# A new layout of the on-chip memory: operands of the dense products below 128 KiB of a partition, most of the rest above

## The reference

```python
# block 1: cond = silu(c); mod = cond @ ada_w + ada_b
h = modulate(rmsnorm(x, norm_mix), sh1, sc1)
x = x + g1 * diff_attention(h, ...)        # 8 heads, softmax(s1) - lam * softmax(s2)
h = modulate(rmsnorm(x, norm_ffn), sh2, sc2)
x = x + g2 * hier_moe(h, ...)              # 16 experts, D -> 512 -> D, two chosen per token
x = rmsnorm(x, norm_final)
# block 2
h = rms_norm(x); x = x + even_mixer(h)     # forgetting attention and multiscale pooling
h = rms_norm(x); x = x + conv_ffn(h)       # D -> 2 x 2816 -> D, convolution of width 3
h = rms_norm(x); x = x + conformer_conv(h) # pointwise, 31 taps, layer norm, pointwise
h = rms_norm(x); x = x + conv_ffn(h)
```

## Time and profile before

| | |
|---|---|
| median of 3 runs | 1865.18 us (1861.98 to 1866.87) |
| span of the profiled execution, first to last instruction | 1865.3 us |
| PE busy | 1803.2 us, 97% of the span, 8492 matmuls |
| PEld, DVE, ACT, POOL busy | 75%, 65%, 49%, 10% |
| mean granted TensorE clock | 0.985 |
| HBM traffic | 143 GB/s over the span |

### The profile page before, as it was taken

The page is one execution under the profiler, slowest core; times in us unless marked ns, Lnnn a source line. Parts: engine busy times, 40 slices in busy tenths (PEclk is TensorE's granted clock), DMA queues, the critical chain, the costliest instruction groups (busy, mean ns, idle before and its releaser), DMA issues.

```text
span 1865.3 us, 26168 instructions
## 1 busy us (share of the span) xinstructions
PE 1803.2 (97%) x8492; PEld 1399.4 (75%) x8492; DVE 1217.4 (65%) x1892; ACT 918.1 (49%) x1402; POOL 186.5 (10%) x219
## 2 busy tenths in 40 slices
PE   7999989899999789999999999999998999999999
PEld 5777667788888667767788888887764788888887
DVE  6777684798898672454577777224898567777422
ACT  3566652578788534564444444215665534444220
POOL 0000000222322100001000000000774000000000
PEclk9999999799999989999999999999999999999999
DMA  9533132999999451110232323321210223332321
GB/s 401 186 94 100 57 124 80 339 361 374 379 372 373 166 199 46 46 46 23 81 102 100 98 93 104 110 90 57 69 59 32 80 79 94 97 101 90 122 92 57
DMA packets 73074, 259.74 MB, mean 139 GB/s; under 512 B 10416, under 2 KB 10544, under 8 KB 71728
## 3 DMA queue, kind: packets, MB, share of 16 engines
q1 hardware_dynamic: 68400, 250.47, 38.5%
q0 software_dynamic: 4608, 8.40, 1.2%
HBM read 254.63 MB, written 12.59 MB: 143 GB/s over the span
## 4 chain that ended last, share of the span: by engine, by line
PE 85%; DVE 6%; issue 4%; ACT 2%; DMA 2%; DVEq 0%; SPq 0%; POOL 0%; POOLq 0%; ACTq 0%
PE ps L1016 18%; PE ps L1018 18%; PE ps L1017 18%; PE ps L1256 3%; PE ps L1257 3%; PE ps L1258 3%; PE ps L1078 2%; PE ps L1276 2%; PE ps L1278 1%; PE ps L1277 1%; PE ps L1099 1%; PE ps L1037 1%; PE ps L1039 1%; PE ps L1038 1%; PE ps L1473 1%
## 5 line engine op out<-in xcount | busy, mean ns | idle before, releaser
L1016 PE MATMUL ps<-h_hi,w_hi 128*128 128x512 f32 x1120 | 448.4, 400 | 1.2 <-DVEq L2267 1.2
L1018 PE MATMUL ps<-h_hi,w_lo 128*128 128x512 f32 x1120 | 437.4, 391 | 0.0
L1017 PE MATMUL ps<-h_lo,w_hi 128*128 128x512 f32 x1120 | 436.9, 390 | 0.0
L124 DVE TENSOR_TENSOR w_lo<-raw,w_hi 128x1024 fp32r<-128x1024 f32 x212 | 266.0, 1258 | 185.4 <-ACT w_hi L119 185.2
L119 ACT ACTIVATE w_hi<-raw 128x1024 fp32r<-128x1024 f32 x212 | 221.5, 1050 | 200.1 <-PE ps L1018 163.9
L1016 PEld LDWEIGHTS ps<-h_hi,w_hi 128*128 128x128 f32 x1120 | 210.7, 188 | 71.5 <-issue 28.4
L1018 PEld LDWEIGHTS ps<-h_hi,w_lo 128*128 128x128 f32 x1120 | 210.6, 188 | 44.4
L1017 PEld LDWEIGHTS ps<-h_lo,w_hi 128*128 128x128 f32 x1120 | 210.9, 188 | 43.9 <-issue 2.4
L163 DVE TENSOR_TENSOR w_lo<-ring,w_hi 128x1024 fp32r<-128x1024 f32 x128 | 149.6, 1219 | 29.4 <-ACT w_hi L159 29.4
L900 ACT ACTIVATE tmp<-ps,param 128x512 f32<-128x512 f32 x88 | 68.7, 780 | 184.7 <-DVE ps L2233 184.7
L2241 DVE SCALAR_TENSOR_TENSOR tmp<-ps,param,tmp 128x511 f32<-128x511 f32 (+1 forms) x176 | 131.8, 749 | 18.9 <-DVE tmp L2241 3.0
(11 more groups left out here) (345 smaller groups left out, 2936.8 us busy)
## 6 DMA issues: line engine op xcount, KB each, us to landing
ring<-in_w_m SPq DMA_DIRECT2D x192, 512.0 KB, 5.4
raw<-in_w_b SPq DMA_DIRECT2D x180, 512.0 KB, 3.5
raw<-in_w_a SPq DMA_DIRECT2D x32, 512.0 KB, 3.6
ada_late<-in_ada_b SPq DMA_DIRECT2D x32, 512.0 KB, 4.2
ada<-in_ada_a SPq DMA_DIRECT2D x8, 1024.0 KB, 20.7
y_tok<-y_dram SPq DMA_DIRECT2D x8, 512.0 KB, 6.9
x<-in_x SPq DMA_DIRECT2D x2, 1024.0 KB, 6.8
h_dram<-h_tok SPq DMA_DIRECT2D x4, 512.0 KB, 2.6
```

What stands on the lines that cost most here:

```text
L124: dve.tensor_tensor(self.lo[:, s, :], self.raw[:, s, :], self.hi[:, s, :].bitcast(F32), ALU.subtract).then_inc(self.lo_done, 1)
L1016: pe.matmul(dst, hi, a_hi, start=first, stop=False, skip_group_check=True)
L1017: pe.matmul(dst, hi, a_lo, start=False, stop=False, skip_group_check=True)
L1018: return pe.matmul(dst, lo, a_hi, start=False, stop=last, skip_group_check=True)
```

## The change

No instruction, wait, size or order is changed: both programs have the same instructions in the same order on each engine. Only where tensors lie is new. `ring` is now a list of 8 slots (`ring_h`, over `h_hi` and `h_lo`) and the 4 slots of `raw`; `ada` is a list of 5 parts low and 3 parts high. Offsets in KiB of a partition, as the two programs allocate them:

| tensor | before | after |
|---|---|---|
| w_hi, w_lo | 92 to 124 | 16.1 to 48.1 |
| h_hi, h_lo | 44 to 76 | 51.9 to 83.9 |
| a_hi, a_lo | 135.8 to 167.8 | 83.9 to 115.9 |
| c_hi | 194 to 210 | 83.9 to 99.9 |
| c_lo | 178 to 194 | 99.9 to 115.9 |
| gv_hi | 135.8 to 179.8 | 83.9 to 127.9 |
| gv_lo | 179.8 to 223.8 | 179.8 to 223.8 |
| m_hi, m_lo | 199.9 to 215.9 | 83.9 to 99.9 |
| e_hi, e_lo | 171.8 to 179.8 | 99.9 to 107.9 |
| hid_hi, hid_lo | 183.8 to 187.8 | 107.9 to 111.9 |
| e_x (two), e_hid | 167.8 to 219.9 | 111.9 to 123.9 |
| v | 157.8 to 173.8 | 83.9 to 99.9 |
| wf_hi, wf_lo | 196.6 to 197.1 | 208.6 to 209.1 |
| glu, diag | 135.8 to 162 | 115.9 to 126.2 |
| const | 16.1 to 24.9 | 127.9 to 136.7 |
| x | 28 to 44 | 139.8 to 155.8 |
| tmp | 124 to 132 | 155.8 to 163.8 |
| junk | 132.8 to 133.8 | 48.9 to 49.9 |
| raw | 76 to 92 | 163.8 to 179.8 |
| ring, 12 slots | 44 to 92 | 51.9 to 83.9 and 163.8 to 179.8 |

The added allocations, in their order, with the lines that stay the same left out:

```diff
+ADA_NEAR = 5
...
-        sp.dma_start(self.ring[:, c], self.src[bass.ds(i, 1), c]).then_inc(self.loaded[c][0], 16)
+        sp.dma_start(self.ring[c], self.src[bass.ds(i, 1), c]).then_inc(self.loaded[c][0], 16)
...
-        const = sb("const", [P, CONST.n])
-        param = sb("param", [P, PARAM.n])
-        x = sb("x", [P, KC, T])
-        with ExitStack() as st:
-            h_hi = sb("h_hi", [P, KC, T], F32R, stack=st)
-            h_lo = sb("h_lo", [P, KC, T], F32R, stack=st)
-            raw = sb("raw", [P, SLOTS, 1024], stack=st)
-        ring = sb("ring", [P, RING, 1024])
         w_hi = sb("w_hi", [P, SLOTS, 1024], F32R)
         w_lo = sb("w_lo", [P, SLOTS, 1024], F32R)
-        tmp = sb("tmp", [P, 4, T])
         ones = sb("ones", [P, P])
...
+            h_hi = sb("h_hi", [P, KC, T], F32R, stack=st)
+            h_lo = sb("h_lo", [P, KC, T], F32R, stack=st)
+        ring_h = sb("ring_h", [P, RING - SLOTS, 1024])
+
+
+        with ExitStack() as st:
+            with ExitStack() as st2:
+                ada_near = sb("ada_near", [P, ADA_NEAR, 2, D], stack=st2)
+                cond = sb("cond", [P, D], stack=st2)
+            v = sb("v", [P, NT, D], stack=st)
+            hd_qk = sb("hd_qk", [P, 2, 2, T], stack=st)
+            at_pt = sb("at_pt", [P, 2, NT, P], stack=st)
+        with ExitStack() as st:
+            m_hi = sb("m_hi", [P, PARTS_M - SLOTS, 1024], F32R, stack=st)
+            m_lo = sb("m_lo", [P, PARTS_M - SLOTS, 1024], F32R, stack=st)
+            e_hi = sb("e_hi", [P, KC, P], F32R, stack=st)
+            e_lo = sb("e_lo", [P, KC, P], F32R, stack=st)
+            hid_hi = sb("hid_hi", [P, FEC, P], F32R, stack=st)
+            hid_lo = sb("hid_lo", [P, FEC, P], F32R, stack=st)
+            e_x = [sb(f"e_x{s}", [P, D], stack=st) for s in range(2)]
+            e_silu = sb("e_silu", [P, FE], stack=st)
+            e_hid = sb("e_hid", [P, FE], stack=st)
+            onehot = sb("onehot", [P, 2, NT, P], F32R, stack=st)
+        with ExitStack() as st:
+            a_hi = sb("a_hi", [P, KC, T], F32R, stack=st)
+            a_lo = sb("a_lo", [P, KC, T], F32R, stack=st)
+            qk2 = sb("qk2", [P, 2, 2, T], stack=st)
+            pt2 = sb("pt2", [P, 2, NT, P], stack=st)
+        with ExitStack() as st:
+            c_hi = sb("c_hi", [P, KC, T], F32R, stack=st)
+            with ExitStack() as st2:
+                act_out = sb("act_out", [P, KC, T], stack=st2)
+            c_lo = sb("c_lo", [P, KC, T], F32R, stack=st)
+            glu = sb("glu", [P, 2, TAPS - 1 + T], stack=st)
+            diag = sb("diag", [P, 2, PE_TAPS, P], stack=st)
+            diag_last = act_out[:, 0:4].rearrange("p a (b c) -> p (a b) c", c=P)
+        gv_hi = sb("gv_hi", [P, FC, T], F32R)
+
+
+        const = sb("const", [P, CONST.n])
+        param = sb("param", [P, PARAM.n])
+        x = sb("x", [P, KC, T])
+        tmp = sb("tmp", [P, 4, T])
+        at_p = tmp
+        raw = sb("raw", [P, SLOTS, 1024])
+        ring = [ring_h[:, c] for c in range(RING - SLOTS)] + [raw[:, c] for c in range(SLOTS)]
...
+        gv_lo = sb("gv_lo", [P, FC, T], F32R)
```

More of the change, by code:

```diff
@@ L158, in split_hi @@
         act.wait_ge(self.used, base + (c + 1))
-        act.activation(self.hi[c % PARTS_M], self.ring[:, c % RING], ACT.Copy).then_inc(self.hi_done, 1)
+        act.activation(self.hi[c % PARTS_M], self.ring[c % RING], ACT.Copy).then_inc(self.hi_done, 1)
     def split_lo(self, dve, base, c):
         dve.wait_ge(self.hi_done, base + (c + 1))
-        dve.tensor_tensor(self.lo[c % PARTS_M], self.ring[:, c % RING], self.hi[c % PARTS_M].bitcast(F32),
+        dve.tensor_tensor(self.lo[c % PARTS_M], self.ring[c % RING], self.hi[c % PARTS_M].bitcast(F32),
                           ALU.subtract).then_inc(self.lo_done, 1)
@@ L202, in build @@
         scrap = sb("scrap", [P, 2])
-        at_p = tmp
         junk = sb("junk", [P, 2, P])
@@ L229, in build @@
         with ExitStack() as st:
-            cond = sb("cond", [P, D], stack=st)
+            h_hi = sb("h_hi", [P, KC, T], F32R, stack=st)
[8 more added lines that the diff above has]
+            at_pt = sb("at_pt", [P, 2, NT, P], stack=st)
@@ L233, in build @@
             with ExitStack() as st2:
[L234 to L237, removed]
+                ada_far = sb("ada_far", [P, KC - ADA_NEAR, 2, D], stack=st2)
             o = sb("o", [P, NT, D], stack=st)
             hd_bias = sb("hd_bias", [P, 2, 2 * T - P], stack=st)
[L241 to L277, removed]
+        ada = [ada_near[:, f] if f < ADA_NEAR else ada_far[:, f - ADA_NEAR] for f in range(KC)]
@@ L282, in build @@
             y_tok = sb("y_tok", [P, 2, NT, D], stack=st)
[L283 to L293, removed]
+            e_y = [sb(f"e_y{s}", [P, D], stack=st) for s in range(2)]
             lg = sb("lg", [P, NT, NG + NE], stack=st)
@@ L304, in build @@
             slot_src, slot_dst = slot_rows[:, 0], slot_rows[:, 1]
[L305 to L308, removed]
+            rms_t = e_x[0][:, 0:4 * P].rearrange("p (n c) -> p n c", n=4)
+            gain_sq = e_x[0][:, 4 * P:4 * P + 32 * KC].rearrange("p (k c) -> p k c", k=KC)
             shift_read, shift_rows = e_x[1], e_y[1]
@@ L310, in build @@
             std_of = tmp[:, 0].rearrange("p (t c) -> p t c", t=NT)
-            router_c = e_y0[:, 10 * (NG + NE):11 * (NG + NE)]
-            r_tok = e_y0[:, 12 * (NG + NE):12 * (NG + NE) + NT]
+            router_c = e_y[0][:, 10 * (NG + NE):11 * (NG + NE)]
+            r_tok = e_y[0][:, 12 * (NG + NE):12 * (NG + NE) + NT]
             gain_diag = [(e_silu, e_hid)[k // 4][:, k % 4 * P:(k % 4 + 1) * P] for k in range(KC)]
-            wr_part = e_y0[:, 0:KC * (NG + NE)].rearrange("p (k n) -> p k n", k=KC)
@@ L315, in build @@
-            wr_sum = e_y0[:, KC * (NG + NE):(KC + 1) * (NG + NE)]
+            wr_part = e_y[0][:, 0:KC * (NG + NE)].rearrange("p (k n) -> p k n", k=KC)
+            wr_sum = e_y[0][:, KC * (NG + NE):(KC + 1) * (NG + NE)]
+        with ExitStack() as st:
+            v2 = sb("v2", [P, NT, T], stack=st)
+            u2 = sb("u2", [P, NG, 16 + T], stack=st)
+            win = sb("win", [P, NG, 16 + T], stack=st)
+            win_tmp = sb("win_tmp", [P, 16 + T], stack=st)
+            w_pool = sb("w_pool", [P, NG, P], stack=st)
+            w_f = sb("w_f", [P, KC, H], stack=st)
+            wf_hi = sb("wf_hi", [P, KC, H], F32R, stack=st)
+            wf_lo = sb("wf_lo", [P, KC, H], F32R, stack=st)
+            nck = sb("nck", [P, 2, T], stack=st)
+            sq2 = sb("sq2", [P, 2, T], stack=st)
+            negc = sb("negc", [P, T], stack=st)
+            r_kept = const[:, CONST["before"].start:CONST["before"].start + T]
+            sel = const[:, CONST["before"].start:CONST["dist"].stop].rearrange("p (h c) -> p h c", h=H)
+            fl = sb("fl", [P, 5, NT * H], stack=st)
+            cq = sb("cq", [P, NT, H], stack=st)
+            gain_q = sb("gain_q", [P, 1], stack=st)
+            fix16 = sb("fix16", [P, 2, 16], stack=st)
@@ L317, in build @@
+        with ExitStack() as st:
+            sig = sb("sig", [P, 2, T], stack=st)
+            prod = sb("prod", [P, 4, T], stack=st)
+            part = sb("part", [P, 2, T], stack=st)
+            conv = sb("conv", [P, KC, T], stack=st)
+        gv_lo = sb("gv_lo", [P, FC, T], F32R)
         h_dram = nc.dram_tensor("h_dram", (T, D), F32, kind="Internal").ap()
@@ L440, in _ @@
             for f in range(KC):
-                sp.dma_start(ada[:, f], a["ada_a"][f]).then_inc(in_ada[f], 16)
+                sp.dma_start(ada[f], a["ada_a"][f]).then_inc(in_ada[f], 16)
                 if f < SLOTS:
@@ L1744, in _ @@
                 dve.wait_ge(in_ada[k], 16)
-                column(ada[:, k, 1], KC + k).then_inc(ada_step, 1)
-                column(ada[:, k, 0], k).then_inc(ada_step, 1)
+                column(ada[k][:, 1], KC + k).then_inc(ada_step, 1)
+                column(ada[k][:, 0], k).then_inc(ada_step, 1)
                 dve.wait_ge(ada_step, 2 * k + 1)
```

## The result

The changed kernel takes 1881.13 us (median of 4 runs, 1877.64 to 1884.81) against 1864.61 (4 runs) for the kernel before: the ratio is 1.0088, 95% interval [1.0073, 1.0104]. It is 16.5 us slower where 10 us faster was forecast. The profiled execution has a span of 1878.6 us and took 1880.38. An execution takes 1.8 us longer than its span wherever both are on record, so the one profiled before, with a span of 1865.3, took some 1867; that its span agreed with the median of 1865.18 was a coincidence.

A forecast was written before the change was run, and what follows sets the result against it. TensorE was taken as the bound, through the pitch of its dense products. Gains of 4.5 (down), 5.2 (experts) and 1.3 (a and c) less 0.5 lost make 10.5 us, so 1865.3 becomes 1854.8, about 1855 us; range 1848.5 to 1861.5.

The forecast's parts named there:

- The step that failed: All dense 512-column products: one pays 6.4 ns more if an operand lies high, above a border between 124 and 135 KiB.
- different loops, PSUM banks and DMA load: Argument against "not the offset" (chance 0.11, 1866 us): four kinds of product that differ in these agree.
- `wf`, taken for a test: Products streaming h with weights at 197 KiB: median 397 ns against 389 for neighbours with low weights, read as showing place.
- Down products: Last FFN, 352 groups of three: the two gv_hi products of each gain 6.4 ns, 4.5 us in all; bounds 0 and 6.8.
- Experts: 1152 expert products, all operands low: 7.4 us gained less 2.1 us for breaks, 5.2 us taken.
- the rival that the DMA bounds this stage: Expert stage: DMA share 1.00 at 377 GB/s holds the gain back, time 1860.0 us; chance 0.07.
- the reserve: End of the expert stage: weights lie ready for 8.9 us, more than the 5.2 us TensorE would run ahead.
- `a` and `c`: 192 products each, in pieces of some 24 between sums of squares: 1.3 us gained, between 0 and 2.5.
- Transposes and `v`: Float32 products: some 432 transposes lose 1.1 us, 256 products of v gain 0.6, together 0.5 us lost.
- Other engines at nothing: Engines other than TensorE: no change in time, as VectorE's subtraction takes 1219 ns into low w_lo and 1218 into high m_lo.
- slower: Fast pitch belongs to particular places of h and w; 3648 products lose 23.3 us, nothing is gained, 1888.6 us; chance 0.05.
- The rule set against the change: TensorE's two read ports are independent and nothing depends on offset; by it alone the change gains 0, time 1865 us.

The follow-up runs named there:

- e3: Kernel before, high tensors left above 128 KiB, region from 136 KiB begun 32 bytes lower and 64 bytes of padding ahead of m_hi: 1851.99 us, ratio 0.9934.
- e1: Changed kernel with scale1 allocated before w_hi, so w_hi and w_lo lie 32 bytes higher: 1854.34 us, ratio to the kernel before 0.9955.
- e2: As e1, plus 160 bytes of padding ahead of gv_lo, which gives it residue 160 too: 1851.37 us, ratio 0.9929.
- e4: Kernel before with scale1 allocated before w_hi, so w_hi, w_lo and tmp lie 32 bytes higher: 1872.47 us, ratio 1.0044.
- e7: Kernel before with four small tensors (128 bytes) allocated before w_hi, w at residue 96 and h at 224: 1884.66 us, ratio 1.0099.
- e6: Kernel before with ones allocated before w_hi, so w_hi, w_lo and tmp lie 512 bytes higher: 1865.53 us, ratio 1.0001.
- e5: Separate kernel without the computation, stretches of 96 products per tensor pair at chosen residues: 226.7 ns a product at equal residues, mostly 233.3 to 233.4 at unequal.

## Why the prediction was wrong

**The step that failed** is where the prediction turns two pitches into a cause: "a dense product pays 233.3 - 226.9 = 6.4 ns if an operand lies high". The price holds for long unbroken rows of products, its condition is wrong: high tensors are as fast as low ones once the residues agree (e3, 226.5 ns with `gv_lo` at 180 KiB), and low ones are slow when they don't (`h` in the changed kernel, 233.3). The table of offsets was read in KiB with one decimal, in which the cause can't be seen, and the only thing in common that was looked for was a threshold. All fast pairs of the kernel before were pairs of residues 224 and 224. The evidence of four groups with "different loops, PSUM banks and DMA load" was one piece of evidence, since their tensors lie in one region that starts at residue 0 (only `m` has another, 192, and it is unequal too). And `wf`, taken for a test, was a scan over eight residues whose one exception stood in the minimum column.

**Down products:** forecast 4.5 us gained, measured 1056 x 2.2 = 2.3. It came with unequal residues (160 and 128, 0 and 128). The changed kernel does not say why mixed unequal residues cost less than the full price. That a product pays for itself alone is wrong as well: in e1 one unequal product in three costs 12.6 ns a group, not 6.4.

**Experts:** forecast 5.2. The `w` slots stay unequal in the changed kernel (402 ns both times), the two `m` slots became equal by chance, and their products gain 1.4 us. With all slots equal, the forecast comes out by the residues: between 400 and 625 us of the kernel before, 225 of some 300 us of this stage, e2 gains 4.7 us and the changed kernel 1.0. In e2 no product waits for a weight slot there, so the rival that the DMA bounds this stage is out: a DMA share of 1.00 was no bound. (The last load is issued at 619.5 and not 619.4 us; the trace has its landing at 624.5, so the reserve is 9.2 us for 8.9.)

**`a` and `c`:** forecast 1.3, measured 0: 395 ns before and after for `a_lo` and `c_lo`. In e1, where their residues are equal, they gain 1.7.

**Transposes and `v`:** forecast 0.5 lost. Measured 0: the transposes of `e_x` have a mean of 281 ns before and 282 after by form, and the starts of all products that are not split, outside of waits and of changes of the clock, differ by 0.05 us in sum.

**Other engines at nothing:** right; VectorE and ScalarE are busy for 1217 and 918 us in both kernels.

**The price in all.** Both traces have the same 8492 products in the same order, so their starts can be compared one by one, leaving out waits and changes of the clock. In the two up stages 2065 `h` products lose 13.6 us, 6.6 ns each, the full price. The 548 in the two attentions lose 1.5 us, 2.8 ns each. They stand there in pieces of mostly 6 or 12 between other products, and behind such a break also products with equal residues have 229 to 235 ns at first; in the first attention they come down to 227 only from the seventh on. The waits of TensorE, which could have hidden the loss as well, are the same in the first attention (5.4 us for `tmp` and 2.8 for `at_m` in both kernels). All `h` and V products together lose 20.7 us and not 23.3; `gv` gives back 2.3 and `m` 1.4, which leaves 17.0 against 16.5 measured.

The two profiled executions are only 13.3 us apart. The rest lies in short stretches at a lower granted clock, which are not at the same place in two executions (from 1425 to 1431 us it is 0.74 in the changed kernel and 1.00 before), and in the waits beside them. The same shortfall of the `h` products shows in the other runs: against the kernel before as measured beside them, 1863.87 and 1865.71, e4 and e7 end 3.1 and 4.4 us under their sums, and the `h` products lose 20.5 and 19.4 us there. In e1 they get back 20.1 us and not 23.3, and `gv` gets nothing instead of 1 to 2; these are the 4 us by which it stays above 1850.

**The rival that came true** is "slower", held at 0.05: the fast pitch belongs to the particular places of `h` and `w`, a bank of finer grain. Of the two causes that it names, the distance of `h` and `w` is out (in e2 and e3 pairs at many distances are all fast, and e6 moves `w` by 512 bytes at no cost) and something of finer grain is what e1 to e7 show. Its 23.3 us were 20.7, and "nothing is gained" was off by 3.7, so the time was 7.5 us under its 1888.6. A look at the residues would have given it the larger chance. What was put against it ("every one of their slots" is fast) does not speak against it: a slot of `w` is 4096 bytes and one of `h` 2048, both multiples of 256.

**The rule set against the change,** that loading weights takes no bandwidth from the running product (the Trainium skill, TensorE: Matmul & The Clock Gate, Step-by-step: what each phase is for), is at odds with the runs at unequal residues: e5 has 226.7 ns a product at equal ones and 233.3 at unequal ones, 0.6 us for 96 products, with nothing else at work. The measurement decides.

## What to carry to other kernels

When one and the same instruction has two durations, list the operands' offsets in bytes and modulo powers of two before believing in regions, and look for the exception in the minimum and maximum columns. In this kernel 32 to 160 bytes of padding, so that all streamed and loaded operands of the split 512-column products start equal modulo 256, are worth 12 to 13 us against the kernel before and 29 to 30 against the change; e2 and e3 are the fastest versions found, and their intervals overlap. Any edit that allocates or frees a small tensor ahead of such operands can give that away, as e4 and e7 show, so the padding belongs in the allocation and not in luck.

## What the runs showed of the hardware

- In a long row of like products, a float32r product of 512 columns has a pitch of 226.5 to 226.9 ns if the offsets of its two operands agree modulo 256 bytes (to 16 bytes at least), and 233.3 to 234.2 otherwise, at granted clock 1.00; a difference of 192 (loaded minus streamed) is an exception with 228.9.
- The half of the memory plays no part: 22.4 us for 96 products for all four combinations of low and high at equal residues.
- Where the residues change from product to product, the pitch lies between 230.0 and 233.4 ns, also if each product's own two operands agree (231.6).
- Behind a break, products with equal residues have 229 to 236 ns at first. In e5 they reach 227 after 2 (`sq`) to 10 (`sa`), in the first attention after 6, so short pieces show less of the difference.
- Products with 256 columns do not gain: 12.1 us for 96 at equal, 11.9 at unequal residues.
